# A two-layer diffusion backbone with routed experts: two of a token's eight expert rows are added by VectorE, and two projection blocks are loaded earlier

## The chip, the cores and the metric

The kernel runs on one NeuronCore of a Trainium2 chip. The metric is the device time of one execution, in microseconds (us). Three runs of the kernel before took 1443.07, 1444.9 and 1446.66 us; their median is 1444.9 us.

The engines are called as the profile calls them: PE is TensorE (matrix products and transposes), PEld its weight loads, DVE is VectorE, ACT is ScalarE, POOL is GpSimd and SP is SyncE, which here only starts transfers (SPq is its queue). Each engine works through its own list of instructions in order, and waits for others on semaphores.

## What is computed

The reference runs two layers over 256 latent tokens and 256 context tokens of width 1024. Each layer has a mixer (attention of two kinds and a long convolution, between one input and one output projection) and then a mixture of experts. What the change touches is the seam from the experts of layer 0 to the projection of layer 1:

```python
# end of layer 0, for the context tokens (xc) and the latent tokens (x) alike
a = jnp.einsum('td,edh->teh', h, w1)
b = jnp.einsum('td,edh->teh', h, w3)
act = (jax.nn.silu(a) * b * gate[..., None])      # gate: non-zero for 8 of 64 experts
routed = jnp.einsum('teh,ehd->td', act, w2)
x = layer_norm(DN_ALPHA * x + g2 * (routed + shared), ln2_g[l], ln2_b[l])
# start of layer 1
hx = modulate(x, sh1, sc1)                        # layer norm, times (1 + scale), plus shift
px = hx @ w                                       # w: 1024 x 2304, the input projection
```

So the 1024 values of a token are a sum over its eight experts' rows, each times its gate, and this sum is multiplied by g2, added to the residual, normalised, normalised again, transposed, and multiplied with w.

## The kernel before

The 512 tokens are four tiles of 128: tiles 0 and 1 are context, 2 and 3 are latent.

**The experts of layer 0.** The 64 experts are worked off in 50 units (`SEQUENCE[0]`), most with one expert, some with two; POOL gathers each unit's tokens (line 2532), PE makes the products (lines 1335 and 1357), and POOL scatters the outputs as rows to a table `scratch_y` in HBM that has eight rows for each token (line 2545). SP loads the weights into eight slots; slots 0 to 3 lie in the buffer `weights`, slots 4 to 7 in `features_h`, `qkv` and other buffers (`expert_w13`, `expert_w2`). A loop behind the 50 units is there for experts with too many tokens. When the last scatter has landed, POOL raises `y_sent`.

**The rows back.** SP then loads the table back, two rows of each token at a time (`rows_back`, 1 MB): a tile has four such pairs, sixteen in all. Pair n goes into `YG[n % 4]`, which are the buffers `a_q`, `b_qk` and the two halves of `features_h`. From the fifth pair on a load waits until the pair that was in its buffer is used. For each tile PE adds up the eight rows (`sum_rows`, line 943): each is multiplied by a diagonal 128 x 128 matrix of the gates (`DIAG`, in `probs_T`), in two halves of 512 columns, into two banks (`SUM`). ACT makes the diagonals (line 1505, shown by the profile as line 1446), up to eight ahead. In the profile a matmul of `sum_rows` has two records, so a pair has eight and the four tiles have 128.

**The norms.** DVE goes through the tiles in batches (0, 1), (2) and (3). For each tile of a batch it multiplies the sum with g2 (line 2413, two halves) and adds it to the residual `X` (line 2415). Then come `post_norm` (lines 1742 to 1843) and `normalise` (down to line 1757, which writes `tokens_h`), and only then the next batch.

**The start of layer 1.** PE transposes tiles 0 and 1 of `tokens_h` (`stream_T`, line 922) after the last `sum_rows`. ACT writes the result with scale and shift into `features_h` (`modulated`, line 1495); since its second half is `YG[3]`, ACT first waits until all pairs are used (line 1506). Then PE makes keys and values of tiles 0 and 1 (`keys_values`, line 951), transposes tiles 2 and 3, makes queries and keys (lines 998 and 951) and the remaining projections (line 1026).

**The projection's weights.** `weights` is also a ring of three slots of 2 MB (`ring_load`), filled in the order of `weight_items`. Item 8 and those behind it belong to layer 1. Items 8 and 9 are loaded between the pairs (after n = 6 and n = 11), item 10 behind the last pair. Item n waits until the last product with item n - 3 is made. `rows_back` and `ring_load` are issued by SP, in the order in which they are written.

## Time and profile before

| | |
|---|---|
| Median of three runs | 1444.9 us |
| The profiled execution | 1440.97 us |
| Its span in the trace | 1439.0 us |
| PE busy | 1288.8 us (90%) |
| DVE busy | 543.9 us (38%) |
| ACT busy | 292.8 us (20%) |
| POOL busy | 301.8 us (21%) |
| DMA, mean over the span | 259 GB/s |

The span runs from the first to the last recorded instruction; the execution is 1.97 us longer. A busy share is an average over stages that have different limits, so it does not say what a change at one place is worth. For that one goes to the place, from 838 us (SP starts the first pair) to 952 us (the last keys and values of layer 1), and reads there what each engine waited for. The chain of waits follows from the end of a piece of work back to what released it; a row there that begins with DMA is a transfer that something waited for.

### The profile page before, as it was taken

Reading aid. Unit: us, or ns where it says so; the run is one execution under the profiler, and the core shown is the slowest. Engines: PE = TensorE matmul, PEld = TensorE weight load, DVE = VectorE, ACT = ScalarE, POOL = GpSimd, SP = SyncE. Lnnn points to the kernel's source line nnn. Section 1 sums busy time; section 2 is a strip of 40 time slices with the busy share of each in tenths; the row PEclk is TensorE's granted clock in tenths of the full one; section 3 lists DMA queues with packets and bytes.
Section 4 is the critical chain, followed back from the end, with each engine's and each line's share of the span. In section 5 each row is a group of like instructions: output and inputs, shape, how many; then the busy total and the mean of one; then the engine's idle time right before and its main releaser. Section 6 shows DMA issues by size and latency. Waiting matters only on the chain.

```text
span 1439.0 us, 19064 instructions
## 1 busy us (share of the span) xinstructions
PE 1288.8 (90%) x6356; PEld 704.4 (49%) x6357; DVE 543.9 (38%) x1327; ACT 292.8 (20%) x715; POOL 301.8 (21%) x394
## 2 busy tenths in 40 slices
PE   5999995999978999989989969899987699999994
PEld 1443452444444666655656724466544354545451
DVE  5303532446575322222323216546446521211124
ACT  0100112323211222222222221212511111111110
POOL 1001002244204233323323300101710411111110
PEclk9999997989988999999999989999988799999997
DMA  9875308535326899999999569340422999999960
GB/s 335 320 277 192 146 0 265 207 144 204 123 100 233 327 374 379 359 369 378 368 383 389 203 260 397 98 166 26 108 103 73 381 401 397 402 408 396 406 250 30
DMA packets 113084, 373.30 MB, mean 259 GB/s; under 512 B 17979, under 2 KB 24381, under 8 KB 104793
## 3 DMA queue, kind: packets, MB, share of 16 engines
q1 hardware_dynamic: 89112, 313.50, 58.1%
q0 software_dynamic: 23008, 55.40, 10.5%
q10 hardware_dynamic: 864, 3.15, 0.5%
q8 instruction: 54, 0.88, 0.3%
q14 instruction: 46, 0.37, 0.1%
HBM read 368.77 MB, written 30.47 MB: 277 GB/s over the span
## 4 chain that ended last, share of the span: by engine, by line
PE 41%; DMA 11%; SPq 9%; DVE 3%; issue 3%; ACT 1%; POOL 0%; POOLq 0%; DVEq 0%; ACTq 0%
PE bank L1335 11%; SPq L647 7%; PE bank L1357 6%; PE bank L1367 5%; DMA weights<-in_exp_w 3%; DMA probs_T<-in_exp_w 3%; PE bank L1323 3%; PE bank L943 3%; DMA qkv<-in_exp_w 2%; PE bank L1145 2%; PE bank L951 2%; PE bank L1036 1%; PE bank L1026 1%; PE bank L1188 1%; DMA a_q<-scratch_y 1%
## 5 line engine op out<-in xcount | busy, mean ns | idle before, releaser
L1335 PE MATMUL bank<-weights,b_qk 128*64 128x256 f32 (+2 forms) x1040 | 160.7, 385 | 1.8 <-DVE b_qk L2295 1.5
L1335 PEld LDWEIGHTS bank<-weights,b_qk 128*64 128x64 f32 (+2 forms) x1040 | 110.7, 147 | 62.3 <-issue 34.5
L2301 DVE TENSOR_TENSOR expert_act<-silu_a,bank 128x128 f32<-128x128 f32 x76 | 21.9, 288 | 309.1 <-ACT silu_a L1658 309.1
L1367 PE MATMUL bank<-tokens_h,a_k 128*128 128x512 f32 x208 | 103.2, 620 | 0.0
L1357 PE MATMUL bank<-weights,expert_act_T 128*64 128x512 f32 (+2 forms) x260 | 92.2, 622 | 10.0 <-DMA weights<-in_exp_w 5.4
L2532 POOL DMA_INDIRECT shift_scale_gate_norm<-scratch_h,gather_index x82 | 85.0, 1037 | 70.6 <-POOL gather_index L2529 43.7
L1335 PE MATMUL bank<-features_h,b_qk 128*32 128x256 f32 (+2 forms) x512 | 95.2, 381 | 0.4
L1323 PE MATMUL bank<-tab,shift_scale_gate_norm 128*128 128x128 f32 x624 | 82.9, 276 | 8.2 <-DMA shift_scale_gate_norm<-scratch_h,gather_index 8.2
L1145 PE MATMUL bank<-weights,features_h 128*128 128x512 f32 x192 | 86.4, 606 | 0.8 <-ACT features_h L1445 0.8
L2485 POOL TENSOR_SCALAR probs<-probs,prob_recip 128x512 f32<-128x512 f32 (+1 forms) x36 | 48.5, 1356 | 176.9 <-DVE prob_recip L2026 176.8
L1658 ACT ACTIVATE silu_a<-bank 128x128 f32<-128x128 f32 x76 | 21.1, 278 | 313.4 <-PE bank L1335 310.3
L1323 PEld LDWEIGHTS bank<-tab,shift_scale_gate_norm 128*128 128x128 f32 x624 | 75.9, 191 | 17.3 <-issue 16.6
L2295 DVE COPY b_qk<-bank 128x512 f32<-128x512 f32 x78 | 54.0, 692 | 72.3 <-PE bank L1323 72.3
L1335 PEld LDWEIGHTS bank<-features_h,b_qk 128*32 128x32 f32 (+2 forms) x512 | 59.6, 140 | 24.3 <-issue 14.9
L2485 POOL TENSOR_SCALAR tokens_h<-tokens_h,prob_recip 128x512 f32<-128x512 f32 (+1 forms) x36 | 50.3, 1408 | 89.2 <-DVE prob_recip L2026 89.2
L1357 PE MATMUL bank<-qkv,expert_act_T 128*32 128x512 f32 (+2 forms) x128 | 57.4, 629 | 9.4 <-DMA probs_T<-in_exp_w 9.4
L1445 ACT ACTIVATE b_qk<-bank 128x512 f32<-128x512 f32 x82 | 49.0, 597 | 79.3 <-PE bank L1323 66.8
L1367 PEld LDWEIGHTS bank<-tokens_h,a_k 128*128 128x128 f32 x208 | 36.5, 192 | 54.9 <-issue 54.7
L2529 POOL COPY gather_index<-token_of_slot 128x1 int32<-128x1 int32 x82 | 16.9, 206 | 220.4 <-PE bank L1323 216.9
L1026 PE MATMUL bank<-features_h,weights 128*128 128x512 f32 (+1 forms) x192 | 62.4, 486 | 0.0
L1335 PE MATMUL bank<-a_q,b_qk 128*128 128x256 f32 (+1 forms) x256 | 62.0, 397 | 0.0
L2545 POOL DMA_INDIRECT scratch_y<-tokens_h,scatter_index x50 | 51.1, 1023 | 44.7 <-POOL scatter_index L2542 43.4
(360 smaller groups left out, 1963.2 us busy)
## 6 DMA issues: line engine op xcount, KB each, us to landing
weights<-in_exp_w SPq DMA_DIRECT2D x195, 512.0 KB, 11.7
features_h<-in_exp_w SPq DMA_DIRECT2D x64, 512.0 KB
qkv<-in_exp_w SPq DMA_DIRECT2D x64, 512.0 KB
shift_scale_gate_norm<-in_ada_w SPq DMA_DIRECT2D x24, 1024.0 KB, 8.1
a_q<-in_exp_w SPq DMA_DIRECT2D x32, 512.0 KB
weights<-in_w_in SPq DMA_DIRECT2D x6, 2048.0 KB
shift_scale_gate_norm<-scratch_mod POOLq DMA_DIRECT2D x16, 512.0 KB, 8.8
c_padded<-in_ada_w SPq DMA_DIRECT2D x8, 1024.0 KB, 6.0
```

The lines of the kernel that those rows point to most:

```text
L647: sp.dma_start(dst, src).then_inc(s, inc)
L1026: mm = pe.matmul(b[:, first:HALF], w[:, k, (f % 4) * P:(f % 4 + 1) * P], HT[:, k, first:HALF], start=k == 0, stop=k == KD - 1)
L1145: mm = pe.matmul(b[:, :], OT[:, c, t * P:(t + 1) * P], wo[:, c, :], start=c == 0, stop=c == KD - 1)
L1323: mm = pe.transpose(XT_PS[k // 4][:, (k % 4) * P:(k % 4 + 1) * P], XG[:, u.slot(), k:D:KD], ident)
L1335: mm = pe.matmul(ab[r, 0:2 * HIDDEN].rearrange("p (m h) -> p m h", m=2), XGT[:, u.slot() % 2, k, r], expert_w13(slot)[:, :, k, :], start=k ...
L1357: mm = pe.matmul(yp[h][r, :], ACTT[:, r], expert_w2(slot)[:, h * HALF:(h + 1) * HALF], start=True, stop=True)
L1367: mm = pe.matmul(ACC[g][h][:, :], GROW[:, u.slot() % 2, g * P:(g + 1) * P], YSB[:, u.slot() % 2, h * HALF:(h + 1) * HALF], start=False, st ...
L1445: return nc.scalar.activation(dst, src, ACT.Copy)
L2295: dve.tensor_copy(XGT[:, u.slot() % 2, 4:8, :], XT_PS[1][:, :].rearrange("p (k t) -> p k t", k=4)).then_inc(L["xT_vector"], 1)
L2485: pool.tensor_scalar(P_[U % 4][:, 0:nk], P_[U % 4][:, 0:nk], RC[:, U % 4:U % 4 + 1], None, ALU.mult).then_inc(p_ready, 1)
L2532: nc.gpsimd.indirect_dma_start(out=XG[:, v, :], out_offset=None, in_=h_dram, in_offset=bass.IndirectOffsetOnAxis(ap=IDXB[:, v:v + 1].bitca ...
L2545: nc.gpsimd.indirect_dma_start(out=y_dram, out_offset=bass.IndirectOffsetOnAxis(ap=IDYB[:, w:w + 1].bitcast(U32), axis=0), in_=YSB[:, w, : ...
```

## The change

**Who adds the rows.** PE adds only rows 0 to 5 of a token (`ON_PE = 6`: three pairs of a tile, in `YG[0]` to `YG[2]`). Rows 6 and 7, the fourth pair, always lie in `YG[3]`. DVE takes them from there: for each half it computes row 6 times its gate plus the bank (a scalar_tensor_tensor, in the place of the multiplication with g2), then for the whole 1024 columns row 7 times its gate plus that, and then multiplies by g2 and adds to the residual. A new semaphore, `rows_added`, counts tiles whose rows 6 and 7 were added. SP waits for it before it reloads `YG[3]`, and ACT waits for all four before it writes `features_h`.

**When the weights are loaded.** For layer 1 the first two projection blocks change places (item 8 is now block 1, keys and values; item 9 is block 0, queries). Items 8 and 10 are loaded while the last expert units of layer 0 run, as soon as the experts that lie in their part of `weights` have been used; item 9 stands between the pairs after n = 6; items 11 and later stand behind the pairs. The loop for too full experts now uses slots 4 to 7.

```diff
+EARLY_ITEMS = (8, 10)
+ON_PE = TOP_K - 2
...
-        items += [("win", l, b) for b in (0, 1, 3, 4, 2)] + [("mixc", l), ("wo", l, 0), ("wo", l, 1)]
+        items += [("win", l, b) for b in ((1, 0) if l else (0, 1)) + (3, 4, 2)] + [("mixc", l), ("wo", l, 0), ("wo", l, 1)]
...
+        rows_added = sem("last_choices_added")
...
-                if n >= len(YG):
-                    sp.wait_ge(choice_used, N - len(YG) + 1)
+                if n >= len(YG) and j < ON_PE:
+                    sp.wait_ge(choice_used, (g - 1) * (ON_PE // 2) + j // 2 + 1)
+                elif n >= len(YG):
+                    sp.wait_ge(rows_added, g)
                 load(YG[N % 4], y_rows[full[g]][:, j:j + 2, :], gathered[N % 4])
...
                         rows_back(l - 1, n)
-                        if n in (6, 11):
+                        if n == 6:
+                            at += 1
                             ring_load(at)
-                            at += 1
+                            at += 2
...
+                if l < DEPTH - 1:
+
+                    for n, held in ((EARLY_ITEMS[0], (EXPERTS - 6, EXPERTS - 5)), (EARLY_ITEMS[1], (EXPERTS - 7, EXPERTS - 6))):
+                        for x in held:
+                            sp.wait_ge(L["y_ps"], 2 * user[x] + 2)
+                        ring_load(n)
...
-                            load_w13(u, i * UNROLL + (loads + u), i * UNROLL + every)
-                            load_w2(u, i * UNROLL + (loads + u), i * (2 * UNROLL) + 2 * every)
+                            load_w13(UNROLL + u, i * UNROLL + (loads + u), i * UNROLL + every)
+                            load_w2(UNROLL + u, i * UNROLL + (loads + u), i * (2 * UNROLL) + 2 * every)
...
-                for j in range(TOP_K):
+                for j in range(ON_PE):
                     N = (g * TOP_K + j) // 2
...
-                    pe.wait_ge(diag_ready, g * TOP_K + j + 1)
+                    m = g * ON_PE + j
+                    pe.wait_ge(diag_ready, m + 1)
...
-                            slot, fills = c - every, i + (-(-(EXPERTS + ALWAYS[l] - (c - every)) // ring_n) + 1)
+                            slot = UNROLL + c - every
+                            fills = i + (-(-(EXPERTS + ALWAYS[l] - slot) // ring_n) + 1)
...
-                    for m in range(TILES * TOP_K):
+                    for m in range(TILES * ON_PE):
...
-                    act.wait_ge(choice_used, TILES * TOP_K // 2)
+                    act.wait_ge(choice_used, TILES * ON_PE // 2)
+                    act.wait_ge(rows_added, TILES)
...
                 for batch in ((0, 1), (2,), (3,)):
                     for t in batch:
-                        dve.wait_ge(choice_used, (t + 1) * TOP_K // 2)
+                        dve.wait_ge(choice_used, (t + 1) * ON_PE // 2)
+                        dve.wait_ge(gathered[3], 16 * (t + 1))
                         for h in (0, 1):
                             cols = slice(h * HALF, (h + 1) * HALF)
-                            tt(MACC[:, t, cols], SUM[t % 2][h][:, :], MODG[:, t // 2, cols], ALU.mult).then_inc(sum_read, 1)
+                            stt(MACC[:, t, cols], YG[3][:, 0, cols], G8[:, t, ON_PE:ON_PE + 1], SUM[t % 2][h][:, :],
+                                ALU.mult, ALU.add).then_inc(sum_read, 1)
                         dve.wait_ge(sum_read, 2 * t + 2)
+                        stt(MACC[:, t, :], YG[3][:, 1, :], G8[:, t, ON_PE + 1:ON_PE + 2], MACC[:, t, :],
+                            ALU.mult, ALU.add).then_inc(rows_added, 1)
+                        dve.wait_ge(rows_added, t + 1)
+                        link(tt(MACC[:, t, :], MACC[:, t, :], MODG[:, t // 2, :], ALU.mult))
                         link(tt(X[:, t, :], X[:, t, :], MACC[:, t, :], ALU.add))
                     post_norm(2, batch)
                     normalise(batch, HN)
```

The order of SP's transfers in the stretch of the pairs, before. Names are buffer<-source with the elements of one transfer; `choice_added` is the semaphore `choice_used` of the code:

```order
L647 DMA features_h<-scratch_y 128x2048 [waits choice_added]
L647 DMA weights<-in_w_in 128x8x512 [waits window_bias_used,bank_filled]
L647 DMA features_h<-scratch_y 128x2048 [waits choice_added]
L647 DMA a_q<-scratch_y 128x2048 [waits choice_added]
L647 DMA b_qk<-scratch_y 128x2048 [waits choice_added]
L647 DMA features_h<-scratch_y 128x2048 [waits choice_added] x2
L647 DMA weights<-in_w_in 128x8x256 [waits bank_filled]
```

And now (`last_choices_added` is `rows_added`; line 650 is the helper that was line 647):

```order
L650 DMA features_h<-scratch_y 128x2048 [waits choice_added]
L650 DMA weights<-in_w_in 128x8x512 [waits bank_filled]
L650 DMA features_h<-scratch_y 128x2048 [waits last_choices_added]
L650 DMA a_q<-scratch_y 128x2048 [waits choice_added]
L650 DMA b_qk<-scratch_y 128x2048 [waits choice_added]
L650 DMA features_h<-scratch_y 128x2048 [waits choice_added]
L650 DMA features_h<-scratch_y 128x2048 [waits last_choices_added]
```

A 2 MB block stands behind pair 6 and ahead of pair 7 in both; the second block between the pairs is gone, and pairs 7 and 11 wait for DVE instead of PE.

DVE's list where tile 2's norms end and tile 3 begins, before:

```order
L1757 TENSOR_SCALAR tokens_h<-residual,mean_var,rstd 128x1024 [waits vector_step]
L2413 TENSOR_TENSOR qkv<-bank6,shift_scale_gate_norm 128x512 [waits vector_step,choice_added]
L2413 TENSOR_TENSOR qkv<-bank7,shift_scale_gate_norm 128x512
L2415 TENSOR_TENSOR residual<-residual,qkv 128x1024 [waits row_sums_read]
L1742 BN_STATS stats<-residual 128x6 [waits vector_step]
```

And now:

```order
L1772 TENSOR_SCALAR tokens_h<-residual,mean_var,rstd 128x1024 [waits vector_step]
L2429 SCALAR_TENSOR_TENSOR qkv<-features_h,choice_gates,bank6 128x512 [waits vector_step,choice_gathered3,choice_added]
L2429 SCALAR_TENSOR_TENSOR qkv<-features_h,choice_gates,bank7 128x512
L2432 SCALAR_TENSOR_TENSOR qkv<-features_h,choice_gates,qkv 128x1024 [waits row_sums_read]
L2435 TENSOR_TENSOR qkv<-qkv,shift_scale_gate_norm 128x1024 [waits last_choices_added]
L2436 TENSOR_TENSOR residual<-residual,qkv 128x1024 [waits vector_step]
L1757 BN_STATS stats<-residual 128x6 [waits vector_step]
```

Each tile has two instructions of 1024 columns more, and the reading of `features_h` for tile 3 (lines 2429 and 2432) stands behind the norms of tiles 0 to 2.

ACT's list at the same seam, before and now, has one more wait at the first write into `features_h`:

```order
L1446 ACTIVATE probs_T<-tab,choice_gates 128x128 [waits y_ps_0,choice_gates_ready]
L1446 ACTIVATE probs_T<-tab,choice_gates 128x128 x7
L1446 ACTIVATE probs_T<-tab,choice_gates 128x128 [waits choice_added] x24
L1495 ACTIVATE features_h<-bank5,mod_columns 128x256 [waits bank_filled,choice_added]
L1495 ACTIVATE features_h<-bank5,mod_columns 128x256
```

```order
L1460 ACTIVATE probs_T<-tab,choice_gates 128x128 [waits y_ps_0,choice_gates_ready]
L1460 ACTIVATE probs_T<-tab,choice_gates 128x128 x7
L1460 ACTIVATE probs_T<-tab,choice_gates 128x128 [waits choice_added] x16
L1509 ACTIVATE features_h<-bank5,mod_columns 128x256 [waits bank_filled,last_choices_added,choice_added]
L1509 ACTIVATE features_h<-bank5,mod_columns 128x256
```

Eight diagonals are gone, and the write waits for `last_choices_added` too.

## Rows read from the trace of the kernel before

**Rows 1.** The chain of waits, 838 to 952 us: start us, us, what

```profile
838.04 4.83 DMA a_q<-scratch_y
...
843.11 16.08 PE bank L943 x32
...
859.20 10.76 DMA features_h<-scratch_y
...
870.01 7.15 PE bank L943 x16
877.17 11.23 DMA a_q<-scratch_y
...
888.45 14.00 PE bank L943 x32
...
902.99 3.77 ACT features_h L1495 x8
...
906.80 14.02 PE bank L951 x32
...
923.93 13.97 PE bank L998 x32
937.90 13.73 PE bank L951 x32
```

**Rows 2.** The timeline, DVE: start us, us, engine, line, what, [idle before]

```profile
859.21 1.29 DVE L2413 TENSOR_TENSOR qkv<-bank,shift_scale_gate_norm 128x512 f32<-128x512 f32 x2 [27.74 <-PE bank L943]
873.82 1.29 DVE L2413 TENSOR_TENSOR qkv<-bank,shift_scale_gate_norm 128x512 f32<-128x512 f32 x2 [12.06 <-PE bank L943]
875.14 1.22 DVE L2415 TENSOR_TENSOR residual<-residual,qkv 128x1024 f32<-128x1024 f32 x1
893.08 1.29 DVE L2413 TENSOR_TENSOR qkv<-bank,shift_scale_gate_norm 128x512 f32<-128x512 f32 x2 [0.25 <-DVE tokens_h L1757]
905.84 1.29 DVE L2413 TENSOR_TENSOR qkv<-bank,shift_scale_gate_norm 128x512 f32<-128x512 f32 x2 [0.15 <-DVE tokens_h L1757]
```

**Rows 3.** The timeline, PE, first three pairs and the transposes behind the last

```profile
843.11 5.76 PE L943 MATMUL bank<-a_q,probs_T 128*128 128x512 f32 x8 [12.37 <-DMA a_q<-scratch_y]
848.71 3.60 PE L943 MATMUL bank<-b_qk,probs_T 128*128 128x512 f32 x8
852.14 7.03 PE L943 MATMUL bank<-features_h,probs_T 128*128 128x512 f32 x16
...
902.28 1.95 PE L922 MATMUL bank<-tab,tokens_h 128*128 128x128 f32 x16
```

**Rows 4.** The timeline, SP's queue, where pair 6, a block and pair 7 are issued

```profile
855.77 0.32 SPq L647 DMA_DIRECT2D features_h<-scratch_y  x1
856.19 0.66 SPq L647 DMA_DIRECT2D weights<-in_w_in  x1
859.20 0.32 SPq L647 DMA_DIRECT2D features_h<-scratch_y  x1
862.64 0.32 SPq L647 DMA_DIRECT2D a_q<-scratch_y  x1
```

**Rows 5.** Windows: us, busy of PE, PEld, DVE, ACT, POOL, then PEclk, DMA share, GB/s

```profile
800.00:820.00 20.00, 19.95 (x91) 14.28 (x90) 5.01 (x9) 5.25 (x12) 7.71 (x13) 1.00 0.45 173
...
836.00:843.00 7.00, 0.00 (x0) 0.00 (x0) 0.00 (x0) 0.76 (x3) 0.00 (x0) 0.50 0.56 206
843.00:848.00 5.00, 4.89 (x7) 2.19 (x8) 0.00 (x0) 0.00 (x0) 0.00 (x0) 0.57 1.02 429
848.00:856.00 8.00, 8.00 (x20) 3.46 (x19) 0.00 (x0) 1.61 (x5) 0.00 (x0) 1.00 0.88 316
```

**Rows 6.** DVE instructions by source line: count, ns min/median/max, first and last start

```profile
L1840 DVE SCALAR_TENSOR_TENSOR residual<-residual,mean_var,shift_scale_gate_norm x4: 1279/1284/1285, 881.4 to 911.7; 128x1024 f32<-128x1024 f32 x4
L1877 DVE SCALAR_TENSOR_TENSOR residual<-residual,filters x12: 691/692/693, 266.0 to 1081.7; 128x512 f32<-128x512 f32 x12
```

**Rows 7.** The page, costliest groups: POOL's gathers and scatters

```profile
L2532 POOL DMA_INDIRECT shift_scale_gate_norm<-scratch_h,gather_index x82 | 85.0, 1037 | 70.6 <-POOL gather_index L2529 43.7
L2545 POOL DMA_INDIRECT scratch_y<-tokens_h,scatter_index x50 | 51.1, 1023 | 44.7 <-POOL scatter_index L2542 43.4
```

More of the change, by code:

```diff
@@ L940, in sum_rows @@
                         pe.wait_ge(sum_read, 2 * (g - 1))
-                    pe.wait_ge(diag_ready, g * TOP_K + j + 1)
+                    m = g * ON_PE + j
+                    pe.wait_ge(diag_ready, m + 1)
                     for h in (0, 1):
-                        mm = pe.matmul(SUM[g % 2][h][:, :], DIAG[:, (g * TOP_K + j) % DIAGONALS, :],
-                                       YG[N % 4][:, j % 2, h * HALF:(h + 1) * HALF], start=j == 0, stop=j == TOP_K - 1)
+                        mm = pe.matmul(SUM[g % 2][h][:, :], DIAG[:, m % DIAGONALS, :],
+                                       YG[N % 4][:, j % 2, h * HALF:(h + 1) * HALF], start=j == 0, stop=j == ON_PE - 1)
                     if j % 2:
@@ L1501, in _ @@
                     act.wait_ge(loop[0]["y_ps"], 2 * len(SEQUENCE[0]))
-                    for m in range(TILES * TOP_K):
+                    for m in range(TILES * ON_PE):
                         if m >= DIAGONALS:
                             act.wait_ge(choice_used, (m - DIAGONALS) // 2 + 1)
-                        copy(DIAG[:, m % DIAGONALS, :], ident, G8[:, m // TOP_K, m % TOP_K:m % TOP_K + 1]).then_inc(diag_ready, 1)
-                    act.wait_ge(choice_used, TILES * TOP_K // 2)
+                        copy(DIAG[:, m % DIAGONALS, :], ident, G8[:, m // ON_PE, m % ON_PE:m % ON_PE + 1]).then_inc(diag_ready, 1)
+                    act.wait_ge(choice_used, TILES * ON_PE // 2)
+                    act.wait_ge(rows_added, TILES)
                 for v in (0, 1):
```

## The prediction, made before the changed kernel ran

> **What bounds the kernel now.** I read the chain of waits first, from the moment at which SP starts the first pair to the end of the last keys and values of layer 1 [rows 1]. Three things take turns. PE adds rows in the three pieces of line 943 (16.08, 7.15 and 14.00 us); between them the chain goes through transfers that something waited for; then ACT writes `features_h` (3.77 us from 902.99) and PE multiplies on from 906.80 with hardly a gap. Since the chain passes through PE's adding, a reader is tempted to price the change by PE's work alone.
>
> The second view is DVE's timeline [rows 2], and it says something that the chain does not. For tiles 0 and 1 DVE waits for PE (27.74 and 12.06 us idle). For tiles 2 and 3 it does not: tile 2 begins at 893.08, 0.25 us behind its own norms, and tile 3 at 905.84, 0.15 us behind its own norms. From 873.82 on DVE has no time to spare. The kernel before hides that, because nobody in layer 1 needs DVE's tile 3 before the keys and values of tiles 0 and 1 are made (906.80 to 920.8).
>
> **What is removed from PE.** A pair costs 852.14 - 848.71 = 3.43 us at the full clock [rows 3]; four pairs go, 13.7 us. Without new waits the last sum would end at 902.28 - 13.7 = 888.6. New waits there are, because transfers do not get faster. Pair 7, issued at 859.20, lands 10.76 us later [rows 1, 4]: ahead of it are pair 6 and the 2 MB block, and this order stays. Its landing stays at 869.96. Pair 8 stands behind it. PE has now finished tile 1 (pairs 4, 5, 6) at 843.11 + 5.60 + 5 x 3.43 = 865.9 and waits for pair 8; at the 400 to 430 GB/s that full windows of this stretch show (429 in [rows 5]) 1 MB takes 2.5 us, so pair 8 lands at 872.5. Three pairs of tile 2 and three of tile 3 take 20.6 us: the last sum ends at 893.1, and PE's transposes, which need tiles 0 and 1 normalised (at 891.9, below), run then. PE gains 902.28 - 893.1 = 9.2 us, not 13.7.
>
> **What is added to DVE.** Per tile: the two halves change from a multiplication into a scalar_tensor_tensor. The nearest rows are both of 512 f32 columns: the pair at line 2413 takes 1.29 us for two [rows 2], and the scalar_tensor_tensor of line 1877 takes 692 ns each [rows 6]; two, one overlapping the other's end, are the same 1.3. So this costs nothing. New are the scalar_tensor_tensor of 1024 columns, 1.28 us by line 1840 [rows 6], and the multiplication by g2 of 1024 columns, 1.22 us by the addition of line 2415 [rows 2], with 0.03 us of hand-over each: 2.56 us per tile.
>
> The Trainium skill speaks against this. Its page "Vector Engine (DVE) Microarchitecture Reference", section "Points that are easy to get wrong", says that a scalar_tensor_tensor with two SBUF sources that are not bf16 runs at half the rate. Line 1840 is just such an instruction (residual and norm rows, both f32 in SBUF), and its 1.28 us for 1024 columns is about the 1.22 us of the plain addition, so the trace does not agree, and I take the row. What the page would make of the sum is a rival below.
>
> **When the last two rows have been added.** This sets the end, by ACT's new wait. DVE's tile 1 starts when pair 7 lands, 869.96, instead of 873.82. Rows 6 and 7 are added at 869.96 + 1.32 + 1.31 = 872.6, the residual at 875.1, against 875.14 + 1.22 = 876.36 before: 1.2 us earlier. The norms of tiles 0 and 1 take what they took, 893.08 - 876.36 = 16.7 us, so tile 2 starts at 891.9. Its pair 11 is long there (issued once tile 1's rows are added, at 872.6). Tile 2 took 905.84 - 893.08 = 12.76 us and takes 15.32: tile 3 starts at 907.2. Pair 15, issued at 894.5 when tile 2's rows are added, lands some 5 us later (the first pair of all took 4.83 on an idle queue [rows 1]), in time. Tile 3's rows are added at 907.2 + 1.32 + 1.31 = 909.8. ACT may write `features_h` from 909.85 instead of 902.99: **6.9 us later**. PE's pairs and the transposes have by then been ready for 14 us; the whole gain of PE and DMA stands in front of this one wait. Queued behind ACT's wait are its eight writes (3.77 us), and PE waits for them.
>
> **The clock.** PE then sits idle from 895 (893.1 plus 1.95 for the transposes) to 909.85 + 3.8 = 913.7, some 18.6 us. After the 12.37 us of idle time ahead of the first pair, the granted clock was at 0.50 (1.2 GHz), stayed low when work began (0.57 in 843 to 848), and was 1.00 (2.4 GHz) from 848 [rows 5]; the first pair took 848.71 - 843.11 = 5.60 us where the next took 3.43 [rows 3]. The keys and values are matmuls of the same 512 columns, so I add 5.60 - 3.43 = **2.2 us**. Before the change PE had waited only 2.57 us there and started warm. The bounds are 0 (it stays warm) and twice this. PE's 6.6 us wait for pair 8 may also cost up to 2.2 us, but that ends in front of ACT's wait and costs nothing.
>
> **What else is moved.** The early loads of items 8 and 10 fall into 800 to 820 us, where DMA is busy 0.45 of the time at 173 GB/s [rows 5]; 4 MB need some 10 us, behind expert weights that have already been issued, and end well before the pairs start at 838. They cost nothing there; a gather or scatter slowed by them has some units of slack, and only the last scatter is on the path, after they have landed. They gain nothing either: the block that they remove stood between pairs that no longer decide. Item 11 is now issued after the last keys and values (951.6) instead of with the queries, but PE needs it only after four of the six products of line 1026, over 13 us later: nothing. The loop for too full experts is not entered: 82 gathers are 50 + 26 units and 2 x 3 ahead, and 50 scatters are the 50 units [rows 7]. Eight fewer diagonals lie beside waiting.
>
> **The sum.** + 6.9 + 2.2 = + 9.1 us. What follows (queries, projections, attention) hangs on this start; its weights and modulation rows are released by the same products, so it moves as a whole, as far as the rows show. The profiled execution would go from 1440.97 to 1450.1 us; against the median of 1444.9 that is **1454 us**, + 0.6%. A measurement of this kernel can tell about 0.3% (4.3 us) from no change.
>
> **The rivals.**
>
> 1. PE and the DMA decide after all (faster). If rows 6 and 7 of tile 3 were added by 893.7, ACT's first write would follow PE's transposes and start 9.2 us earlier than before: 1435.7. It decides from the point at which DVE's chain is shorter than PE's, and that needs 16 us less on DVE between 870 and 910; the order puts the norms of tiles 0 to 2 (16.7 + 10.2 us) ahead. For it speaks only the chain before, which names PE and DMA. Chance 0.05.
> 2. Pair 7 lands early enough that DVE starts tile 1 at PE's 865.9, not at 869.96. The chain moves up 4.1 us: + 5.0, 1449.9. For it: SP asks for the pair slightly earlier (rows of tile 0 are added at about 858.5 against 859.20). Against: the bytes ahead of it are the same. With the clock staying up as well it is + 2.8, within 0.3%. Chance 0.12.
> 3. PE's clock stays up over the pause: + 6.9, 1451.8. Against it is the 0.50 at 836 to 843. Chance 0.10.
> 4. Pairs 8 and 9 are asked for 3.4 us earlier than before and share the engines with pair 7, which lands up to 2.5 us later: + 11.6, 1456.5. Chance 0.08.
> 5. The half rate for two f32 sources of SBUF. Only line 2432 has two; 1.28 us more for tiles 1, 2 and 3: + 12.9, 1457.8. It is the page's rule named above. Chance 0.03.
> 6. Something later absorbs most of the delay, a transfer or POOL's work that was late anyway: 1444.9 to 1449. I found no such wait behind 906 in the chain, where PE follows on PE. Chance 0.04.
>
> My forecast has the rest, 0.58. The range reaches from the rival with the early pair to the half rate: 1449 to 1458. Slower by over 0.3% is the forecast, rivals 3 to 5 and half of rival 2: 0.85. Within 0.3%: the other half and rival 6, 0.10. Faster: 0.05.
>
> **What would show it.** Right: 96 records at the sum of rows instead of 128, with a wait of some 6 us for pair 8; DVE's tile 1 at 870, tile 2 at 892, tile 3 at 907; ACT's first write into `features_h` at 910, released by DVE (line 2432); a pause of PE of over 15 us before the keys and values, and a granted clock of 0.5 behind it. Wrong: an ACT write that follows directly on the transposes near 894, or DVE idle between tiles 2 and 3; either means that the time of the pairs decides and that the change gains. If all this appears and the time is still that of before, the delay was absorbed behind 952 us.

## The result and the profile after

The changed kernel took 1454.94 us (median of 7 runs, 1450.53 to 1457.45), the kernel before 1443.07 us on the same chip (7 runs, 1438.76 to 1446.66). The ratio is 1.007, with a 95% interval of 1.005 to 1.0089: **slower by 7 to 13 us**. The profiled execution took 1455.23 us, its span is 1453.4 us.

The chain of waits of the kernel after, over the same seam (start us, us, what), answers [rows 1]:

```profile
841.84 5.01 DMA a_q<-scratch_y
...
847.09 12.46 PE bank L956 x24
...
862.33 9.88 DMA features_h<-scratch_y
...
872.34 1.42 DVE qkv L2429 x2
...
894.41 1.42 DVE qkv L2429 x2
...
909.94 1.42 DVE qkv L2429 x2
911.38 1.30 DVE qkv L2432
912.75 3.76 ACT features_h L1509 x8
916.56 17.02 PE bank L964 x32
...
936.69 13.97 PE bank L1011 x32
```

Before, PE's additions and transfers filled the chain; now PE leaves it after the first tile and DVE holds it for 40 us, from pair 7's landing to ACT's write. That is the turn that the prediction named.

DVE's timeline, which answers [rows 2] (at the end, the idle time before and who ended it):

```profile
859.58 1.41 DVE L2429 SCALAR_TENSOR_TENSOR qkv<-features_h,choice_gates,bank 128x512 f32<-128x512 f32 x2 [24.31 <-PE bank L956]
872.34 1.41 DVE L2429 SCALAR_TENSOR_TENSOR qkv<-features_h,choice_gates,bank 128x512 f32<-128x512 f32 x2 [7.52 <-DMA features_h<-scratch_y]
873.78 1.28 DVE L2432 SCALAR_TENSOR_TENSOR qkv<-features_h,choice_gates,qkv 128x1024 f32<-128x1024 f32 x1
875.10 1.23 DVE L2435 TENSOR_TENSOR qkv<-qkv,shift_scale_gate_norm 128x1024 f32<-128x1024 f32 x1
876.36 1.23 DVE L2436 TENSOR_TENSOR residual<-residual,qkv 128x1024 f32<-128x1024 f32 x1
894.41 1.41 DVE L2429 SCALAR_TENSOR_TENSOR qkv<-features_h,choice_gates,bank 128x512 f32<-128x512 f32 x2 [0.35 <-DVE tokens_h L1772]
```

Tile 1 waits for pair 7, tile 2 for nothing but DVE's own norms. The new instruction of 1024 columns takes 1.28 us.

PE's timeline, which answers [rows 3], and ACT's write:

```profile
847.09 5.58 PE L956 MATMUL bank<-a_q,probs_T 128*128 128x512 f32 x8 [12.55 <-DMA a_q<-scratch_y]
...
874.75 5.40 PE L956 MATMUL bank<-a_q,probs_T 128*128 128x512 f32 x8 [4.91 <-DMA a_q<-scratch_y]
...
897.15 1.95 PE L934 MATMUL bank<-tab,tokens_h 128*128 128x128 f32 x16
916.56 17.00 PE L964 MATMUL bank<-weights,features_h 128*128 128x512 f32 x32 [17.46 <-ACT features_h L1509]
```

```profile
912.75 3.75 ACT L1509 ACTIVATE features_h<-bank,mod_columns 128x256 f32<-128x256 f32 x8 [28.44 <-DVE qkv L2432]
```

PE ends its sums and starts the transposes at 897.15, is idle for 17.46 us behind them, and then needs 17.0 us for keys and values that took 14.00 before. The windows (us, busy of PE, PEld, DVE, ACT, POOL, then PEclk, DMA share, GB/s) show the clock behind that, as [rows 5] did for the first pair:

```profile
904.00:916.00 12.00, 0.00 (x0) 0.00 (x0) 11.21 (x21) 3.25 (x8) 0.00 (x0) 0.50 0.00 0
916.00:920.00 4.00, 3.44 (x4) 1.52 (x5) 3.62 (x12) 0.51 (x2) 0.00 (x0) 0.50 0.00 0
920.00:924.00 4.00, 4.00 (x8) 1.63 (x7) 3.69 (x11) 0.00 (x0) 0.00 (x0) 0.67 0.00 0
924.00:940.00 16.00, 14.65 (x47) 7.51 (x46) 3.26 (x9) 3.02 (x6) 3.26 (x6) 1.00 0.19 63
```

**Where the time went.** One measure is used for all kernels below: the *seam*, from SP's first pair to the end of the keys and values of tiles 0 and 1. Before it is 920.84 - 838.04 = 82.80 us, after 933.60 - 841.84 = 91.76: **+ 8.96**. The rest of the profiled difference (1455.23 - 1440.97 = 14.26) lies outside it. The pairs begin 3.80 us later; what delays them lies before 801 us, and the early loads are issued at 805.89. And near the end of the program stands something that the prediction doesn't have. The chain before:

```profile
1412.61 3.63 PE bank L1367 x8
1416.24 4.42 issue
1420.66 0.54 PE bank L1418
```

and after:

```profile
1423.44 3.63 PE bank L1380 x8
1427.07 7.89 issue
1434.96 0.65 PE bank L1432
```

Between the last product of layer 1's experts and the small count matmuls behind the loop for too full experts, PE stands for 4.42 us before and **7.89 us after**; nothing in the trace ends this wait. The change has no line there. I call it the tail gap: + 3.47. Between seam and tail gap after is 1.9 us shorter (489.84 against 491.77 us from the end of the keys and values to the last eight matmuls). 3.80 + 8.96 - 1.93 + 3.47 = 14.3. The 1.93 us come from single traces and stay open.

### The profile page after: what moved, and what is told of

Read it like the earlier page. It is cut to its first block, busy times and chain, and to the rows that moved or that the text cites. A ratio compares the mean times of both kernels' runs of the same rounds, so it can differ in the third digit from the quotient of the medians.

```text
span 1453.4 us, 19001 instructions
## 1 busy us (share of the span) xinstructions
PE 1280.0 (88%) x6324; PEld 700.5 (48%) x6325; DVE 554.4 (38%) x1335; ACT 289.8 (20%) x707; POOL 301.1 (21%) x394
## 4 chain that ended last, share of the span: by engine, by line
PE 39%; SPq 12%; DMA 7%; DVE 6%; issue 3%; ACT 1%; POOL 0%; POOLq 0%; DVEq 0%; ACTq 0%
PE bank L1348 11%; SPq L650 10%; PE bank L1370 6%; PE bank L1380 5%; PE bank L1336 3%; DMA qkv<-in_exp_w 2%; PE bank L964 2%; PE bank L1158 2%; DMA weights<-in_exp_w 2%; DMA probs_T<-in_exp_w 1%; PE bank L1049 1%; PE bank L1039 1%; SPq L784 1%; SPq L775 1%; PE bank L1201 1%
## 5 line engine op out<-in xcount | busy, mean ns | idle before, releaser
L1158 PE MATMUL bank<-weights,features_h 128*128 128x512 f32 x192 | 84.3, 593 | 0.8 <-ACT features_h L1459 0.8
L964 PE MATMUL bank<-weights,features_h 128*128 128x512 f32 x128 | 59.4, 622 | 17.5 <-ACT features_h L1509 17.5
## 6 DMA issues: line engine op xcount, KB each, us to landing
weights<-in_exp_w SPq DMA_DIRECT2D x195, 512.0 KB, 11.9
```

The source lines that it names most:

```text
L964: mm = pe.matmul(b[:, :], HT[:, k, t * P:(t + 1) * P], w[:, k, :], start=k == 0, stop=k == KD - 1)
L1158: mm = pe.matmul(b[:, :], OT[:, c, t * P:(t + 1) * P], wo[:, c, :], start=c == 0, stop=c == KD - 1)
```

## The experiments

My theory: the seam's + 9 us are DVE's additions behind its norms, 6 us by waiting and 3 us by PE's clock; the early loads do nothing. Rivals: the early loads and the block between the pairs cost it; the time of the pairs decides; the clock is a bystander. The tail gap needed a theory of its own.

The experiments ran in three sessions, each with the kernel before beside it; its medians there were 1443.71, 1444.11 and 1442.79 us. A ratio to before is measured within a session. A time "below after" compares sessions, and a difference of 1 or 2 us in it says little.

### Each half of the change alone

`rows_only` is after with before's order of the weights:

```diff
-                        if n == 6:
-                            at += 1
+                        if n in (6, 11):
                             ring_load(at)
-                            at += 2
+                            at += 1
...
-                    for n, held in ((EARLY_ITEMS[0], (EXPERTS - 6, EXPERTS - 5)), (EARLY_ITEMS[1], (EXPERTS - 7, EXPERTS - 6))):
-                        for x in held:
-                            sp.wait_ge(L["y_ps"], 2 * user[x] + 2)
-                        ring_load(n)
```

> The change's first part alone: VectorE adds rows 6 and 7, but the projection blocks are loaded as before (one 2 MB block behind pair 6, one behind pair 11, one behind pair 15). I measure the seam from SP's first pair to the end of the keys and values of tiles 0 and 1: 82.8 us before, 91.8 us after the change. Theory (VectorE's chain and ScalarE's wait for it set the end): pair 7 still lands behind one block, VectorE's tiles start at the same distances, so the seam is 91 to 92.5 us and the kernel 8 to 11 us slower than before, like the whole change. The sum of rows ends some 4 us later than with early loads and nobody minds. Rival (the early loads carry part of the result): without them the sum ends later and pushes the end, seam 95 us or more.

1453.76 us (6 runs), 1.0067 times before (1.0054 to 1.0081). Seam 91.9, the same as after. The whole loss is in this half. The sum of the rows ends 6.9 us later than in after (62.24 against 55.31 us behind SP's first pair; 4 were expected), without an effect on the seam. PE's pause is only 10.72 us here, and the keys and values still take 16.95.

`early_only` is before with the early loads and without the rows on DVE (the same lines, the other way round, in before).

> The change's second part alone: TensorE adds all eight rows, but items 8 and 10 are loaded during the last expert units and item 9 behind pair 6. Theory: the wait for pair 12 (1.6 us of idle TensorE before) goes, the one for pair 7 stays, nothing is added: seam 81 to 81.5 us against 82.8, kernel 1 to 2 us faster than before, hardly measurable. Rival (early loads disturb gathers and scatters of the last units, and this is where the 3.8 us come from by which the first pair started later in the changed kernel's trace): first pair 3 us or more later than before, seam 81 us, kernel 2 us slower.

1444.5 us (12 runs), 1.0006 times before (0.9993 to 1.002): no difference, though 1 to 2 us were expected. The gain came and went. ACT writes `features_h` 63.37 us after SP's first pair instead of 64.95, so 1.58 us earlier; but the keys and values take 15.70 us:

```profile
907.97 15.70 PE L959 MATMUL bank<-weights,features_h 128*128 128x512 f32 x32 [2.55 <-ACT features_h L1504]
```

```profile
895.00:905.00 10.00, 10.00 (x35) 5.21 (x34) 9.26 (x19) 0.84 (x2) 0.00 (x0) 1.00 0.01 2
905.00:912.00 7.00, 4.45 (x10) 1.95 (x9) 6.43 (x16) 2.91 (x7) 0.00 (x0) 0.76 0.00 0
```

The granted clock is 1.00 up to 905 and 0.76 over 905 to 912, about a pause of only 2.55 us. Before had the same pause, 2.57 us, and its 14.00 us of products behind it ran at full clock. So the seam stays at 82.89, where 81 to 81.5 were expected. A short pause can fall on either side. The rival's sign, a later first pair, is there too (840.79 against 838.04), but rows_only has it without early loads (841.41), and the time does not move.

### The block between pairs 6 and 7

`item9_late` is after with item 9 behind pair 14, so that pair 7 has no 2 MB ahead of it:

```diff
-                        if n == 6:
+                        if n == 14:
                             at += 1
                             ring_load(at)
                             at += 2
```

> The changed kernel with one edit: the remaining block (item 9) is loaded behind pair 14, not behind pair 6. Theory (pair 7's landing starts VectorE's chain, because a 2 MB block stands ahead of it): pair 7 lands 4 to 5 us sooner, VectorE's tile 1 starts when TensorE has summed it, 4.1 us earlier relative to the first pair, and the whole chain follows: seam 87.5 to 88 us against 91.8, kernel 4 us faster than the changed one and still about 5 us slower than before. Rival (ScalarE's wait has another cause, or the chain has slack): seam stays at 91 to 92 us.

1450.49 us (6 runs), 1.0043 times before (1.0028 to 1.0058), 4.4 below after. DVE's tile 1 starts 28.0 us after SP's first pair instead of 30.5, ACT's write comes at 68.39 instead of 70.91, and the seam is 88.77: 3.0 shorter, of which 2.5 are the earlier start. Expected were 4.1 us for DVE's tile 1: it now starts when PE has summed it, as told, but pair 7 had come earlier in after than the expectation took it to. The chain from pair 7 over DVE to ACT is real, and what its head gains, 2.5 us, arrives at ACT's write whole.

### The clock alone

`keep_warm` is after with 19 matmuls of 512 columns in PE's pause (nothing of the computation is left out; what they write is overwritten):

```diff
                     if l and v == 0:
+                        pe.wait_ge(sum_read, 2 * (TILES - 1))
+                        for _ in range(19):
+                            pe.matmul(bank(("kv", l, 0))[:, :], ident, TAB[:, 0:HALF], start=True, stop=True)
```

> The changed kernel with 19 matmuls of 128x512 between the transposes of tiles 0 and 1 and the keys and values; their results are overwritten and never used. They fill TensorE's pause of 17.5 us with 16.3 us of work. Theory (the pause costs the clock): the granted clock is 1.00 when the keys and values begin, these take 14.0 us instead of 17.0, ScalarE's write into features_h comes at the same time: seam 88.8 us against 91.8, kernel 3 us faster than the changed one. Rival (the 17.0 us have another cause, such as reading features_h just written): 17.0 us again, seam 91.8 us.

```profile
897.27 16.47 PE L1001 MATMUL bank<-tab 128*128 128x512 f32 x38
914.87 14.00 PE L964 MATMUL bank<-weights,features_h 128*128 128x512 f32 x32 [1.13 <-ACT features_h L1512]
```

The write stays where it was (70.97), the keys and values take 14.00 us again, and the seam is 88.80: 2.96 shorter, the clock's share, measured alone, in one trace of each. The time is 1445.78 us (12 runs), 1.0013 times before (1.0002 to 1.0025): 9.2 below after, three times what the seam gave (8.2 by the two ratios). The trace shows one more part: the tail gap is 4.47 us instead of 7.89. Seam and gap are 6.4; the rest lies within the intervals of the two ratios.

### DVE's order

`adds_first` has DVE add tile 3's last rows before it normalises tile 2 (the same instructions in another order):

```diff
+                for t in (0, 1):
+                    last_rows(t)
+                    to_residual(t)
+                norms((0, 1))
+                last_rows(2)
+                to_residual(2)
+                last_rows(3)
+                norms((2,))
+                to_residual(3)
+                norms((3,))
```

> The changed kernel with VectorE's list in another order: tile 3's rows 6 and 7 are added before the norms of tile 2, not behind them. All work is the same. Counted from SP's first pair, ScalarE wrote features_h at 70.9 us in the changed kernel and at 65.0 before. Theory (the place of tile 3's additions behind 10.3 us of norms is what delays ScalarE): pair 15 lands at 60.4, its rows are added at 63.1, ScalarE writes at 63.2. Then VectorE's norms of tiles 2 and 3 end at 86.2 and TensorE goes on with the queries at 89.6 against 94.9 in the changed kernel and 85.9 before: 5 us faster than the changed one, still 3 to 4 us (plus the 3.4 us at the kernel's end) slower than before. Rival (the additional 10 us of VectorE work decide, wherever the additions stand): queries no earlier than 93.

1448.67 us (12 runs), 1.0033 times before (1.0019 to 1.0047), 6.3 below after. ACT's write moves from 70.91 to 63.05 us, the queries' start from 94.85 to 89.25; 63.2 and 89.6 were expected. The seam is 82.7 us, as short as before's. Of the 7.9 us on ACT only 5.6 reach the queries, since PE now waits there for DVE's norms of tiles 2 and 3 (3.11 us). DVE now waits 2.50 us for pair 15:

```profile
901.08 1.41 DVE L2431 SCALAR_TENSOR_TENSOR qkv<-features_h,choice_gates,bank 128x512 f32<-128x512 f32 x2 [2.50 <-DMA features_h<-scratch_y]
```

DVE works as much here as in after (554.1 and 554.4 us), so these 5.6 us were the place of two rows in its list. But the queries still start 3.4 us later than before's 85.89, and the kernel is still slower than before: DVE has more to do until the norms of tile 3 end.

### The tail gap

`pad64` puts 64 empty instructions (`pe.nop()`) into PE's pause of after.

> The changed kernel with 64 empty instructions of TensorE in its 17.5 us pause behind the transposes, so that its program has about as many instructions as before (the change took 64 out). In the traces with the shorter program TensorE stands still for 7.6 to 7.9 us between the last expert's matmuls and the last four of line 1432, in those with the old length or a longer one for 4.4 to 4.6 us, and nothing that the profile shows released it. Theory (it depends on where the code behind the skipped loop lies): 4.5 us again, the seam unchanged at 91.8 us, kernel 3.4 us faster than the changed one. Rival (it comes from what ran before): 7.8 us again and no gain.

1453.88 us (6 runs), tail gap 7.35. As a test it tells nothing: in the built program PE has 4608 instructions with and without these 64 lines. It is a second sample of after, and as such it shows how far two executions differ: its keys and values take 15.46 us, where after's took 17.00, and its seam is 90.2 instead of 91.8. The count of instructions in the built programs was the useful part, for it sorts all traces that I had. A matmul of f32 counts as one in it and leaves four entries in the trace, two matmuls and two weight loads.

| kernel | PE instructions | tail gap, us |
|---|---|---|
| after, rows_only, item9_late, adds_first, pad64, combined_plain | 4608 | 7.89, 7.86, 7.60, 7.38, 7.35, 7.05 |
| before | 4630 | 4.42 |
| early_only | 4628 | 4.55 |
| keep_warm | 4627 | 4.47 |
| combined_warm | 4622 | 4.20 |

PE jumps over the loop's body there. The Trainium skill, page "Runtime: NRT & Kernel Launch", section "Instruction fetch mechanics", says that instructions are fetched ahead in blocks of 16 KiB, 256 instructions, and that a taken branch to a block outside the window waits for a fetch. By that rule the place of the code behind the branch would set the gap, and a shift by 256 would change nothing. I count an f32 matmul as four of the 256, as its entries suggest. Then before, early_only, keep_warm and combined_warm have that code 70, 68, 76 and 56 instructions behind its place in after. Four kernels try the rule (the fourth, `combined_tiny16`, is told further down). They put one-column matmuls into PE's pause ahead of the first pair:

```diff
                 if l:
+                    for _ in range(16):
+                        pe.matmul(SUM[0][0][:, 0:1], ident, TAB[:, 0:1], start=True, stop=True)
                     for g in range(TILES):
                         sum_rows(g)
```

> The kernel after, with 16 one-column matmuls (64 PE records or so, some 1.1 us) put into PE's 12 us pause ahead of the first pair; their result is overwritten, nothing of the computation is left out. They put back the number of instructions that the change takes out of PE's program (16 f32 matmuls) and leave the seam alone. In the six traces of programs with the change's number of PE instructions the engine stands 7.05 to 7.89 us between its last eight matmuls on tokens and the count matmuls behind the skipped extra turns; in the four with 14 to 22 instructions more (before, early_only, keep_warm, combined_warm) it stands 4.20 to 4.55 us. Theory position (where the code behind the taken branch lies decides that gap): gap 4.2 to 4.6, the seam from SP's first pair to the end of keys/values of tiles 0 and 1 unchanged at 91.8, median 3.3 below after, about 1451. Rival clock or data (the gap comes of what PE does in the seam, not of the code's place): gap 7.0 to 7.9, median about 1454.

> The kernel after with 64 one-column matmuls in the same pause (256 instructions of PE, one whole block of code if blocks hold 256); nothing is left out. Theory position with a period of one block: as without them, gap 7.0 to 7.9, seam 91 to 92, median about 1454. Rival (more code behind the branch simply shortens the gap, or any filling does): gap 4.2 to 4.6, about 1451.

> The kernel before with 47 one-column matmuls in the same pause: its code behind the skipped turns then lies, counted modulo 256 instructions, within two of where it lies in after. The rows of the change are not there: eight of eight rows are added on TensorE. Nothing is left out. Theory position: the tail gap is 7.0 to 7.9 instead of 4.42, the seam stays at 82.8, the median is 3.3 above before, about 1447. Rival (the gap comes of the change itself, not of the code's place): gap 4.2 to 4.6, median 1444.

The chain of after_tiny16 at the end of the program:

```profile
1417.71 3.63 PE bank L1382 x8
1421.35 4.12 issue
1425.46 0.90 PE bank L1434 x2
```

and that of before_tiny47, which has nothing of the change:

```profile
1430.48 3.63 PE bank L1369 x8
1434.11 6.89 issue
1441.00 1.04 PE bank L1420 x2
```

With 16 matmuls (64 instructions) more, after has the short gap, 4.12 us; with 64 (256) more it has the long one again, 7.23; and before, moved by 47 (70 + 188 = 258) to within two of after's place modulo 256, has the long one, 6.89. **The gap belongs to the code's place.** The transfers in the 11 us up to the end of the gap point to the mechanism. In after:

```profile
q8 instruction: 2, 0.03, 1.5%
q14 instruction: 1, 0.01, 0.3%
```

and in before:

```profile
q8 instruction: 1, 0.02, 0.8%
```

Two packets of 16 KB on queue 8 in each of the eight kernels with a long gap, one in each of the six with a short one. Their times fit: in all fourteen traces one packet starts 0.7 to 1.1 us ahead of the gap, in the eight a second starts 1.9 to 3.0 us into it, and the gap ends 3.4 to 4.3 us after the last of them has ended. (The short ones have another packet some 8.5 us ahead of the gap, outside the 11 us.) No semaphore ties the packets to PE's wait; it is their number and their times that go with it. Trace and page agree in the block's size and in the wait; that a second block costs some 3 us more is what the runs add. The page has no price for it.

after_tiny16 took 1449.87 us (6 runs), 1.0048 times before (1.0031 to 1.0065), 5.1 below after, where 3.3 were expected; by the ratios, 1.0048 against 1.007, it is 3.2. Its seam is 91.65, unchanged. The other two need a correction, because I had the fillers' price wrong:

```profile
839.12 27.44 PE L972 MATMUL bank<-tab 128*128 128x1 f32 x128 [5.61 <-issue]
```

A record with one column takes 214 ns here (27.44 / 128), half as long as one with 512 columns at full clock (3.43 us for the eight records of a pair, 429 ns each). So 64 of them don't fit in the pause: the first pair starts 25.62 us after SP's transfer instead of 5.25, and of the 1474.29 us 20.4 are that delay; 1453.9 is left, after's time. before_tiny47 took 1461.13 us and its pairs start 13.3 us late; 1447.8 is left, where 1447 was expected. Less the delays, their seams are 92.1 and 82.9 us, those of after and of before.

### A version that gains

`combined_plain` takes what the runs taught: all four tiles' rows are added before the norms of tiles 2 and 3, which go as one batch; pair 15 goes into free space in `qkv`; item 9 stands behind pair 14; ACT waits for three tiles of `rows_added` before the half of `features_h` that is `YG[3]`, and for the fourth before it writes `qkv`.

```diff
+                if n == 15:
+                    sp.wait_ge(sums_free, 1)
+                    load(PAIR15, y_rows[full[g]][:, j:j + 2, :], pair15_in)
+                    return
...
+                norms((0, 1))
+                last_rows(2)
+                last_rows(3)
+                to_residual(2)
+                to_residual(3)
+                norms((2, 3))
```

> A version meant to keep what the change frees: item 9 behind pair 14, pair 15 into the first half of qkv (free once tiles 0 and 1 are in the residual), tile 3's rows added before the norms of tile 2, norms of tiles 2 and 3 in one batch, ScalarE waiting for three tiles' additions before the second half of features_h and for the fourth only before it writes qkv. Theory: the first write into features_h follows the transposes at 53, keys and values start at 55 to 57 and end at 69 to 71 from SP's first pair, VectorE is ready with tile 3 at 77.5, queries start at 81 to 82 against 85.9 before: 4 us faster than before at this place, but 3.4 us are lost at the kernel's end, since the program is short: 0 to 1 us faster than before. Rival (VectorE's chain is longer than I count): queries at 85 or later, kernel 3 us slower than before.

1443.63 us (12 runs), 1.0007 times before (0.9992 to 1.0022). The keys and values start at 55.44, as expected, 13.3 us earlier than before. But the queries start at 83.58, where 81 to 82 were expected (before 85.89): they wait for the norms of tiles 2 and 3, PE is idle for 9.24 us, and the clock is lost there instead (queries 16.07 us instead of 13.97, the transposes ahead of them 3.68 instead of 1.95). The c-projections start 113.22 us after SP's first pair, before's 113.43. What was won on PE is lost on DVE and the clock, and the tail gap is 7.05.

`combined_tiny16` adds 16 one-column matmuls, so the code's place alone.

> combined_plain with 16 one-column matmuls ahead of the first pair, so with the code's place put back but without the full-width fillers of combined_warm. Nothing is left out. Theory position: tail gap 4.2 to 4.6 instead of 7.05, seam mark (SP's first pair to the start of the c-projections) 113.2 as in combined_plain, median 2.9 below it, about 1440.8: most of combined_warm's 5.3 are the code's place. Rival (its fillers earned it by the clock): gap as it may be, the median stays near 1443.6 and only full-width fillers help.

1440.54 us (13 runs), 0.9982 times before (0.9968 to 0.9995), 3.1 below combined_plain, tail gap 4.20: as the place theory said, at 1440.8. The c-projections start at 113.83, 0.6 later than expected, because the keys and values took 15.70 us behind a pause of 2.56. (The profiled execution is the slowest of the 13, 1449.1 us; its pairs start at 845.69, the latest of all traces.)

`combined_warm` has full-width fillers instead, six ahead of the first pair and eight behind the keys and values:

```diff
+                    for _ in range(6):
+                        pe.matmul(SUM[0][0][:, :], ident, TAB[:, 0:HALF], start=True, stop=True)
...
+                        b = start(("hT", l, 1, 1, 0))
+                        for _ in range(8):
+                            pe.matmul(b[:, :], ident, TAB[:, 0:HALF], start=True, stop=True)
```

> combined_plain with matmuls that nobody reads in TensorE's two pauses: 6 ahead of the first pair, 8 behind the keys and values of tiles 0 and 1. Theory (clock): the first pair takes 3.5 us instead of 5.6 and what follows the second pause runs at the full clock; this moves VectorE's chain up by 2 us: queries at 79 to 80 from SP's first pair against 85.9 before; the program has its old length again, so the pause at the end is 4.5 us: 5 to 7 us faster than before, which is 0.35 to 0.5%. Rival (filling delays the first pair, or the clock gains nothing): no faster than combined_plain.

**1438.3 us (12 runs), 0.9962 times before (0.9947 to 0.9977)**: faster than both kernels. Its fillers earned less than planned.

```profile
841.74 3.60 PE L963 MATMUL bank<-a_q,probs_T 128*128 128x512 f32 x8
...
904.35 7.03 PE L1015 MATMUL bank<-tab 128*128 128x512 f32 x16
914.78 3.68 PE L941 MATMUL bank<-tab,tokens_h 128*128 128x128 f32 x16 [3.40 <-DVEq L2462]
919.67 16.01 PE L1023 MATMUL bank<-weights,features_h 128*128 128x512 f32 x32 [1.21 <-ACT features_h L1521]
```

The first pair ran warm, but the next transfers were then waited for. Behind the keys and values the fillers ended 3.40 us before the transposes, the clock was at 0.60 over 912 to 920, and the queries took 16.01 us and started at 83.37, not at 79 to 80. The c-projections start at 112.95, 0.27 earlier than in combined_plain. Of the 5.3 us below that kernel the tail gap (4.20) is 2.85; the rest stays open. Nor is it shown that the full-width fillers beat 16 one-column matmuls: the intervals of the two ratios (0.9947 to 0.9977, and 0.9968 to 0.9995) overlap.

## Why the prediction was right, point by point

- **Who decides.** Right. DVE's tiles, ACT's wait for `rows_added` and PE's pause came as told; rows_only, item9_late and adds_first each moved the end through this chain.
- **The wait, + 6.9.** Measured + 5.96 (70.91 against 64.95). The step that was off is pair 7's landing, "its landing stays at 869.96", 31.9 us behind SP's first pair: it came after 30.4, and DVE began at 30.5. SP asked 0.7 us earlier, since the rows of tile 0 were used earlier, and the transfer took 9.88 us instead of 10.76. That is a third of rival 2. The other way went "this costs nothing": two halves take 1.41 us, not 1.29, because a scalar_tensor_tensor with one source in a bank is slower than the multiplication (742 to 748 ns against 678 to 692); with the hand-overs 0.5 us along the chain. - 1.4 + 0.5 is the difference.
- **The clock, + 2.2.** Measured 3.0, by the 17.0 us and again by keep_warm; in the second sample of the same program it was 1.5, in rows_only 2.9, in item9_late 2.6. The price was taken from eight records behind a shorter pause; here the granted clock was still 0.67 over 920 to 924. It lay inside the bounds of 0 and 4.4. In the profiled execution both errors cancel: 9.1 forecast, 8.96 measured.
- **The rule of the half rate.** Line 2432 takes 1.28 us, line 2435 for as many columns 1.23. The page's rule doesn't hold here, and rival 5 is out.
- **The early loads: nothing.** Right, and for the reason given: with DVE's chain in front, the pairs no longer decide (seam 91.9 in rows_only, without the early loads, and 91.8 in after, with them). In the kernel before, where the pairs do decide, they gave ACT 1.6 us, and the clock took them (early_only 1.0006). Item 11, issued later, cost nothing either: the queries and the c-projections start 8.96 us later than before, like the end of the seam.
- **PE's wait for pair 8.** Forecast 6.6, measured 4.91, with the clock lost behind it (5.40 us for the pair), and without any cost, as told.
- **The other rivals.** Pair 7 landed earlier, not later (rival 4), the clock fell to 0.50 (rival 3), ACT's write came nearly 14 us behind the end of the transposes instead of with them (rival 1), and behind the seam nothing absorbed the delay but, at most, the 1.93 us (rival 6).
- **What was missed: the tail gap, + 3.5.** "It moves as a whole" is false by this. Taking 16 matmuls out of PE's program moved the code behind a branch some 500 us later in the execution. The medians fit it: 8.96 + 3.47 = 12.4, and 11.9 was measured. By themselves they would not show it, since the ratio's interval, 7 to 13 us, holds 9.1 as well; the traces show it (after, after_tiny16 and before_tiny47), and after_tiny16's ratio, 1.0048 instead of 1.007, agrees. The forecast was + 9.1 on a base of 1444.9; before's median in this comparison was 1443.07. That 1454 came so close to 1454.94 is luck: the forecast difference was 2.8 us short of the measured one, and the base was 1.8 us too high.
- **The start of the pairs** (838.04 and 841.84) is, as far as the traces show, no effect of the change. In the other twelve traces it lies between 836.30 and 845.69, for before_tiny47 at 841.67. A difference of two single traces ahead of a seam has to be looked up in others before it is explained.

## What to carry to other kernels

Before moving work from the engine that the chain names to one that is 38% busy, read that engine's own timeline at the place: if it waits for nothing there, what is added to it delays whoever reads its result, and the order of its list (which result is needed first) can matter more than the amount: here 5.6 of 9.0 us at the queries. A longer pause of PE can cost twice, by its length and by the clock behind it (1.5 to 3.0 us here). In a program with branches, compare the gaps behind them in both traces before crediting the change with the whole difference; here 16 matmuls more or less moved such a gap by 3 us.

## What the runs showed of the hardware that I had not expected

- PE stood 4.1 to 4.6 us at a taken branch with one 16 KB instruction transfer there and 6.9 to 7.9 us with two, depending on where the code behind it lay (14 traces).
- A pause of 2.55 us was enough for the granted clock to fall in early_only (0.76 over 905 to 912, products 15.70 us), while 2.57 us cost before nothing (14.00 us). The same pause of 2.56 us stands in four more traces: the products took 15.70 us behind it in combined_tiny16 and 14.00 in combined_plain, combined_warm and before_tiny47. In combined_warm 3.40 us of pause behind 7 us of full-width fillers cost 2.0 us on the queries and 1.7 on the transposes ahead of them.
- A scalar_tensor_tensor of 512 f32 columns with one source in a bank takes 742 to 748 ns; with both in SBUF [rows 6] has 692 ns.
- A one-column f32 matmul with its weight loads takes 0.43 us (two records of 214 ns): as a filler it costs half of what 512 columns cost at full clock, not the 0.07 us that I had reckoned with. It did not bring the clock up either. A window of after_tiny64 in which PE does only this:

```profile
845.00:866.00 21.00, 21.00 (x101) 21.00 (x100) 0.00 (x0) 0.00 (x0) 0.00 (x0) 0.50 0.35 146
```

PE is busy throughout and the granted clock stays at 0.50 (1.2 GHz); the first pair behind it takes 5.80 us, as behind an idle pause.

- An empty instruction in the source need not be one in the program.
